# A two-block transformer on one core: the forget gates' columns go beside the rotated key's, and products of two heads alternate between array halves

## What is computed

```python
def _token_mixer(x, ...):
    z = x @ w_in                     # [256, 1024] @ [1024, N_IN]
    c_q, c_kv, k_rope, sb_qkv, conv_in, fox_qkv, fox_f, gate_logits = _split_cols(z)
    y_a = _mla(c_q, c_kv, k_rope, ...)                  # 4 heads, 96-wide queries and keys
    y_b = _stick_breaking(*_split_heads(sb_qkv))        # 4 heads of 64
    y_c = _conformer_conv(conv_in, ...)                 # 31 taps, a layer norm
    y_d = _forgetting_attention(*_split_heads(fox_qkv), fox_f, b_forget)
    gates = sigmoid(gate_logits + b_gate)
    merged = sum over branches of (y @ w_branch) * gates
    return merged @ w_o

def _forgetting_attention(q, k, v, forget_logit, b_forget):
    log_f = log_sigmoid(forget_logit + b_forget)        # 256 tokens, 4 heads
    c = cumsum(log_f)
    logits = q @ k * scale + c[query] - c[key]          # then causal softmax, then @ v
```

## Time and profile before

| | |
|---|---|
| median of 3 runs | 2617.33 us (2615.58 to 2617.4) |
| profiled execution | 2615.79 us, span of its instructions 2614.0 us |
| PE busy | 2441.6 us, 93% of the span |
| DVE, ACT busy | 676.6 us, 450.1 us |
| share of the chain that ended last | PE 71%, DMA 23%, DVE 3%, ACT 2% |
| third mixer, fourth mixer | about 1455 to 1700 us and 2033 to 2270 us of the span |

### The profile page before, as it was taken

The page is one execution under the profiler, slowest core; times in us unless marked ns, Lnnn a source line. Parts: engine busy times, 40 slices in busy tenths (PEclk is TensorE's granted clock), DMA queues, the critical chain, the costliest instruction groups (busy, mean ns, idle before and its releaser), DMA issues.

```text
span 2614.0 us, 28378 instructions
## 1 busy us (share of the span) xinstructions
PE 2441.6 (93%) x11488; PEld 1398.9 (54%) x11488; DVE 676.6 (26%) x1400; ACT 450.1 (17%) x814; POOL 0.2 (0%) x4
## 2 busy tenths in 40 slices
PE   7999999888889999988888999999999999999998
PEld 5775743333336673333333777774444777874443
DVE  3653321111003232101001533134112533042113
ACT  3141110000002121000000133102111242112111
POOL 0000000000000000000000000000000000000000
PEclk9999999999999999999999899999999999999999
DMA  9348669999997138999999532246999232148994
GB/s 402 132 188 366 250 282 428 428 429 428 428 427 289 73 129 335 429 428 428 429 428 427 215 129 97 97 192 239 425 422 416 110 129 97 65 193 331 426 421 187
DMA packets 53941, 769.64 MB, mean 294 GB/s; under 512 B 5984, under 2 KB 6496, under 8 KB 7008
## 3 DMA queue, kind: packets, MB, share of 16 engines
q1 hardware_dynamic: 53568, 768.17, 71.2%
q10 hardware_dynamic: 288, 0.26, 0.1%
HBM read 767.36 MB, written 1.05 MB: 294 GB/s over the span
## 4 chain that ended last, share of the span: by engine, by line
PE 71%; DMA 23%; DVE 3%; ACT 2%; issue 1%; SPq 0%; ACTq 0%; DVEq 0%
DMA slab<-in_experts 22%; PE psum L400 14%; PE psum L432 13%; PE psum L1930 8%; PE psum L1920 8%; PE psum L1967 7%; PE psum L1902 6%; PE psum L696 4%; PE psum L503 1%; DMA slab<-in_dense 1%; PE psum L1240 1%; PE psum L1953 1%; PE psum L626 0%; PE psum L1944 0%; PE psum L746 0%
## 5 line engine op out<-in xcount | busy, mean ns | idle before, releaser
L1920 PE MATMUL psum<-slab 128*64 128x512 f32 x2048 | 461.1, 597 | 77.6 <-DMA slab<-in_experts 73.8
L400 PE MATMUL psum<-slab 128*128 128x256 f32 (+6 forms) x1560 | 389.1, 406 | 12.2 <-ACT slab L2480 7.0
L1967 PE MATMUL psum<-slab 128*64 128x512 f32 x1536 | 359.5, 603 | 2.6 <-ACT slab L1998 2.6
L432 PE MATMUL psum<-slab 128*128 128x256 f32 x1504 | 345.4, 391 | 11.8 <-DVE slab L2770 6.6
L1920 PEld LDWEIGHTS psum<-slab 128*64 128x64 f32 x2048 | 142.1, 137 | 390.3 <-issue 274.7
L400 PEld LDWEIGHTS psum<-slab 128*128 128x128 f32 (+2 forms) x1560 | 272.9, 188 | 121.6 <-issue 70.6
L432 PEld LDWEIGHTS psum<-slab 128*128 128x128 f32 x1504 | 294.1, 196 | 60.9 <-issue 8.8
L1902 PE MATMUL psum<-slab 128*128 128x256 f32 x1024 | 249.3, 385 | 1.2 <-DVE slab L2020 1.2
L1930 PE MATMUL psum<-slab 128*64 128x512 f32 x1024 | 225.3, 592 | 0.0
L1902 PEld LDWEIGHTS psum<-slab 128*128 128x128 f32 x1024 | 183.2, 189 | 72.7 <-issue 50.3
L2010 DVE TENSOR_TENSOR slab<-psum,slab 128x512 f32<-128x512 f32 (+1 forms) x64 | 35.7, 558 | 691.6 <-PE psum L1920 502.3
(11 more groups left out here) (429 smaller groups left out, 1565.0 us busy)
## 6 DMA issues: line engine op xcount, KB each, us to landing
slab<-in_experts SPq DMA_DIRECT2D x288, 2048.0 KB, 20.2
slab<-in_dense SPq DMA_DIRECT2D x73, 2048.0 KB, 9.2
slab<-in_dense SPq DMA_DIRECT2D x2, 1680.0 KB, 16.8
slab<-in_vec SPq DMA_DIRECT2D x1, 2571.5 KB, 33.0
slab<-in_dense SPq DMA_DIRECT2D x1, 1328.0 KB, 27.6
slab<-in_dense SPq DMA_DIRECT2D x2, 640.0 KB, 13.9
slab<-in_xT SPq DMA_DIRECT2D x1, 1024.0 KB, 8.4
out<-slab SPq DMA_DIRECT2D x2, 512.0 KB, 2.6
```

The source lines that it names most:

```text
L400: ins = mm(out_ap, lhs, rhs, start=(n == 0), stop=(n == len(pairs) - 1), skip_group_check=True)
L432: ins = mm(psum[:, b, S * j:S * j + S], narrow(s, width)[:, k, c0 + P * j:c0 + P * j + P], src[:, k, :], start=(k == 0), stop=(k == KD - 1 ...
L1920: ins = mm(psum[CAP * e:CAP * e + CAP, n, :], xg[:, k, CAP * e:CAP * e + CAP], sl(w, KD)[:, e * (KD // 2) + i, :], start=(k == 0), stop=(k ...
L1967: ins = mm(psum[CAP * e:CAP * e + CAP, 2 + half, :], hidT[:, f, CAP * e:CAP * e + CAP], w, start=(f == 0), stop=(f == fc - 1), skip_group_ ...
```

## The change

1. Forget gates. They are computed with their four weight columns as the stationary side, into PSUM rows 0 to 3 of bank 3, and their eight products alternate with the eight of the rotated key. ACT copies the result, four rows of 256, to `lfr`. After the units of stick-breaking queries and keys two PE transposes turn it to tokens on partitions, as unit 7, and ACT copies it to `lf` as before. The list `MIX2_FREE` is unchanged.
2. Values of `mla` and `fox`: for each pair of heads (0 and 1, 2 and 3) both first products, then both second ones.
3. Logits of `mla` and `fox`: order of places 0, 2, 1, 3, which for `fox` is heads 0, 1, 2, 3.
4. Stick breaking: its logits' and values' products by pairs of heads in the same manner.

```diff
     def pe_logits(self, q, qk):
         for t in range(NT):
-            for j in range(H):
+            for j in (0, 2, 1, 3) if self.beside == 2 else range(H):
...
     def pe_values(self, q, v_of, out_of):
         q.e.wait_ge(sems["turned_read"], q.due("turned_read"))
-        for j in range(H):
-            h = self.order[j]
-            o = out_of(h)
-            mm(o, v_of(h, 0), self.pT[:, j, 0:2, :]...)
-            ins = mm(o[:, P:S], v_of(h, 1), self.pT[:, j, 2, :], ...)
+        for first in range(0, H, self.beside):
+            own = [list(self.order).index(h) for h in range(first, first + self.beside)]
+            for j in own:
+                h = self.order[j]
+                mm(out_of(h), v_of(h, 0), self.pT[:, j, 0:2, :]...)
+            for j in own:
+                h = self.order[j]
+                ins = mm(out_of(h)[:, P:S], v_of(h, 1), self.pT[:, j, 2, :], ...)
...
+lfr = view(MA0 + 3 * S, S)
...
 pe_mix2_in:
-    accumulate(psum[CH:96, b, S:2 * S], [(narrow(s, 420)[:, k, 384:416], xT[:, k, :]) for k in range(KD)])\
-        .then_inc(sems["unit_done"], 1)
-    b = u.bank()
-    for t in range(NT):
-        ins = accumulate(psum[:, b, H * t:H * t + H],
-                         [(xT[:, k, P * t:P * t + P], narrow(s, 420)[:, k, 416:420]) for k in range(KD)])
+    for k in range(KD):
+        for rows_, c0, n in ((slice(CH, 96), 384, 32), (slice(0, H), 416, H)):
+            ins = mm(psum[rows_, b, S:2 * S], narrow(s, 420)[:, k, c0:c0 + n], xT[:, k, :], start=(k == 0), stop=(k == KD - 1), ...)
     ins.then_inc(sems["unit_done"], 1)
     s = slot(q)
     for n in range(2):
         pe_features(u, s, xT, 2 * P * n)
+    b = u.bank()
+    u.need(4)
+    for t in range(NT):
+        ins = nc.tensor.transpose(psum[:, b, H * t:H * t + H], lfr[0:H, P * t:P * t + P], ident[0:H, 0:H])
+    ins.then_inc(sems["unit_done"], 1)
...
 act_mix2_in:
     A.activation(ckv, psum[:, 3, 0:S], ACT.Copy)
+    A.activation(lfr[0:H, :], psum[0:H, 3, S:2 * S], ACT.Copy)
...
-    act_unit(q, 4, lf, n=NT * H, shape=NT)
-    act_unit(q, 5, sbq, shape=2)
-    act_unit(q, 6, sbk, shape=2)
+    act_unit(q, 4, sbq, shape=2)
+    act_unit(q, 5, sbk, shape=2)
+    act_unit(q, 6, lf, n=NT * H, shape=NT)
...
 pe_sb:
-    for h in range(H):
-        half = slice(CH * (h % 2), CH * (h % 2) + CH)
-        mm(psum[:, h, 0:S], sbk[half, h // 2, 0:P], sbq[half, h // 2, :], start=True, stop=True)
-        ins = mm(psum[:, h, S:3 * P], sbk[half, h // 2, P:S], sbq[half, h // 2, P:S], start=True, stop=True)
+    for first in (0, 2):
+        for part in range(2):
+            for h in (first, first + 1):
+                half = slice(CH * (h % 2), CH * (h % 2) + CH)
+                ins = mm(psum[:, h, S * part:S + P * part], sbk[half, ...], sbq[half, ...], start=True, stop=True)
...
 dve_forget:
-    q.e.wait_ge(sems["lin_read"], q.due("lin_read", 3))
+    q.e.wait_ge(sems["lin_read"], q.due("lin_read", 5))
```

More of the change, by code:

```diff
@@ L732, in build, with __init__ @@
         class Attention:
-            def __init__(self, at, order, scale, turn=4, first=0):
+            def __init__(self, at, order, scale, turn=4, first=0, beside=1):
                 self.lg = view(at, NT, H, S)
@@ L738, in __init__ @@
                 self.nmax, self.sums = view(at + 3584, NT, H), view(at + 3592, NT, H)
-                self.order, self.scale, self.turn, self.first = order, scale, turn, first
+                self.order, self.scale, self.turn, self.first, self.beside = order, scale, turn, first, beside
             def pe_logits(self, q, qk):
                 for t in range(NT):
-                    for j in range(H):
+                    for j in (0, 2, 1, 3) if self.beside == 2 else range(H):
                         lhs, rhs = qk(j, t)
@@ L786, in pe_values @@
                 q.e.wait_ge(sems["turned_read"], q.due("turned_read"))
-                for j in range(H):
-                    h = self.order[j]
-                    o = out_of(h)
-                    mm(o, v_of(h, 0), self.pT[:, j, 0:2, :].rearrange("p a b -> p (a b)"), start=True, stop=False,
-                       skip_group_check=True)
-                    ins = mm(o[:, P:S], v_of(h, 1), self.pT[:, j, 2, :], start=False, stop=True, skip_group_check=True)
+                for first in range(0, H, self.beside):
+                    own = [list(self.order).index(h) for h in range(first, first + self.beside)]
+                    for j in own:
+                        h = self.order[j]
+                        mm(out_of(h), v_of(h, 0), self.pT[:, j, 0:2, :].rearrange("p a b -> p (a b)"), start=True, stop=False,
+                           skip_group_check=True)
+                    for j in own:
+                        h = self.order[j]
+                        ins = mm(out_of(h)[:, P:S], v_of(h, 1), self.pT[:, j, 2, :], start=False, stop=True, skip_group_check=True)
                 ins.then_inc(sems["attn_ready"], 1)
@@ L2354, in build @@
         MA0 = A0 + 8544
-        mla = Attention(MA0, range(H), 96.0 ** -0.5)
-        fox = Attention(MA0, (0, 2, 1, 3), CH ** -0.5)
+        mla = Attention(MA0, range(H), 96.0 ** -0.5, beside=2)
+        fox = Attention(MA0, (0, 2, 1, 3), CH ** -0.5, beside=2)
         sz, sl_, sn = (view(MA0 + 1536 * j, H, 3 * P) for j in range(3))
         mla_sq = view(MA0, 3, S)
+        lfr = view(MA0 + 3 * S, S)
         mt = view(MA0, 2, H, S)
@@ L2377, in pe_mix2_in @@
             accumulate(psum[:, b, 0:S], [(narrow(s, 420)[:, k, 256:384], xT[:, k, :]) for k in range(KD)])
-            accumulate(psum[CH:96, b, S:2 * S], [(narrow(s, 420)[:, k, 384:416], xT[:, k, :]) for k in range(KD)])\
-                .then_inc(sems["unit_done"], 1)
-            b = u.bank()
-            for t in range(NT):
-                ins = accumulate(psum[:, b, H * t:H * t + H],
-                                 [(xT[:, k, P * t:P * t + P], narrow(s, 420)[:, k, 416:420]) for k in range(KD)])
+            for k in range(KD):
+                for rows_, c0, n in ((slice(CH, 96), 384, 32), (slice(0, H), 416, H)):
+                    ins = mm(psum[rows_, b, S:2 * S], narrow(s, 420)[:, k, c0:c0 + n], xT[:, k, :], start=(k == 0), stop=(k == KD - 1),
+                             skip_group_check=True)
             ins.then_inc(sems["unit_done"], 1)
@@ L2606, in pe_sb @@
             q.e.wait_ge(sems["attn_read"], q.due("attn_read"))
-            for h in range(H):
-                half = slice(CH * (h % 2), CH * (h % 2) + CH)
-                mm(psum[:, h, 0:S], sbk[half, h // 2, 0:P], sbq[half, h // 2, :], start=True, stop=True)
-                ins = mm(psum[:, h, S:3 * P], sbk[half, h // 2, P:S], sbq[half, h // 2, P:S], start=True, stop=True)
+            for first in (0, 2):
+                for part in range(2):
+                    for h in (first, first + 1):
+                        half = slice(CH * (h % 2), CH * (h % 2) + CH)
+                        ins = mm(psum[:, h, S * part:S + P * part], sbk[half, h // 2, P * part:P * part + P], sbq[half, h // 2, P * part:],
+                                 start=True, stop=True)
             ins.then_inc(sems["sb_pre"], 1)
@@ L2622, in pe_sb @@
             q.e.wait_ge(sems["sb_prob"], q.due("sb_prob"))
[L2623 to L2627, removed]
+            for first in (0, 2):
+                for t in range(NT):
+                    for h in (first, first + 1):
+                        o = branch_out(h)
+                        ins = mm(o[:, P * t:], vsf[:, t, CH * h:CH * h + CH], sz[:, h, S * t:S + P * t], start=(t == 0), stop=(t == 1),
+                                 skip_group_check=True)
             ins.then_inc(sems["attn_ready"], 1)
@@ L2757, in dve_merge @@
         def dve_merge(q, l):
-            q.skip("lin_read", 11)
+            q.skip("lin_read", 9)
             q.skip("unit_done", 16)
```

## The result

| | before | changed kernel |
|---|---|---|
| median, same chip, 7 runs each | 2615.58 us | 2604.15 us (2596.92 to 2607.76) |
| ratio | | 0.9948 (95%: 0.9933 to 0.9963) |
| profiled execution | 2615.79 us | 2599.33 us |
| mean granted clock over its span | 0.985 | 0.989 |

The change saves 13.6 us by the ratio (9.7 to 17.5), where 11.4 was forecast. The time forecast, 2605.9 us, lies 1.8 us above the median of the seven runs. So there is something to explain on both counts: what the sum got right, and why single executions of one program lie 10.8 us apart.

A forecast was written before the change was run, and what follows sets the result against it. PE was taken as the bound, by the chain in order of time. In-projection 9.6, values 1.3 and 0.2, logits 0.3 sum to 11.4 us: 2615.79 to 2604.4, plus 1.5 for the median, 2605.9 us; range 2602.5 to 2611.

The forecast's parts named there:

- the low end: Whole kernel: 2602.5 us, from 1.6 us more by values, logits and transposes and 1.7 us more by the clock.
- a fall of the clock avoided once more, at half of the 3.4 us: In-projection clock: 1.7 us beyond the sum, half of the 3.4 us (1.2 + 2.2) that one fall cost.
- In-projection, 9.6 us: Third and fourth mixers: moved forget gates save 6.5 us and 3.1 us, of which 2.2 us is clock in the third.
- The gates are free beside the key: In-projection: sixteen gate rows run at once with the rotated key's sixteen, stretch stays 3.7 us; bound 3.5 us each mixer.
- second rival: In-projection: gates' products don't run beside the key's, 3.5 us come back twice, gain 4.4 us, 2612.9 us; chance 0.07.
- Program order: Values and stick-breaking logits: if matmuls run strictly in turn, 5.2 us gained instead of 1.8, 2602.5 us; not adopted.
- Transposes: In-projection: two PE transposes of the gates cost 0.6 us together (bounds 0.3 and 1.0), their wait nothing.
- fourth rival: Slower: PE waits at the transposes or `mla_norm` for ACT and DVE, 8.3 us in each mixer, 2622.5 us; chance 0.03.
- `fox` values: Attention: the new head order brings them from 2.17 to 1.51 us, 0.66 us in each mixer, 1.3 us.
- `fox` logits: Attention: drop from 2.11 to about 1.8 us but give nothing; PE's idle time before L778 grows.
- third rival: Experts: the gain is lost where transfers run at a share of 0.98, time near 2617 us; chance 0.05.
- First rival: In-projection: the clock gives nothing back, 1.2 + 2.2 us are lost, gain 8.0 us, 2609.3 us; chance 0.24.

The follow-up runs named there:

- run of the pairs alone: The kernel before with only the new order of heads in values and logits, forget gates unchanged; 2612.8 us, ratio 0.9989.
- runs in blocks: Changed kernel, key and gate products alternating in blocks: eight products 2608.28 us, two 2603.27 us, four 2602.7 us.
- run in blocks: Changed kernel with the eight products of the rotated key first, then the eight of the gates; 2608.28 us, ratio 0.9974.
- on one tile: Changed kernel with the gates' products on the rotated key's array columns, result in another PSUM bank; 2609.5 us, ratio 0.9976.

## Why the sum came out, and why the low end did not hold

The mechanism was right, and the sum of the work holds. What failed is the low end, 2602.5 us, and in it one step: "a fall of the clock avoided once more, at half of the 3.4 us", 1.7 us, as all that the clock could give beyond the sum. The profiled execution, which is also the median of the first three, lies 3.2 us below it. Its span is 16.3 us shorter than that of before: 9.6 + 1.4 + 0.4 = 11.4 of the terms that I had, 3.2 by falls that are missing at the two `fox` waits, 2.5 by a clock that comes back sooner in the 96 rows ahead of the latent key, less 0.9 in the rest. The step allowed 1.7 us for what was 5.7 in this execution. Of that, much is luck: over seven executions the median is 2604.15 us, inside the range.

- **In-projection, 9.6 us: right.** It is 6.48 + 3.16 = 9.6 in the profiled pair. Elsewhere it is split otherwise: the run of the pairs alone takes 1504.40 - 1476.72 = 27.68 us where the changed kernel takes 22.84, 4.8 in each mixer, 9.7 in both. I had read one mixer with a fall of 3.4 us and one with none; two other profiles have some 1.7 in each. The sum is the same by chance of the one profile I had.
- **The gates are free beside the key: right**, 3.59 us for both, 7.04 on one tile. The Trainium skill says in "TensorE: Matmul & The Clock Gate", Part 3, that a weight load overlaps a running matmul only where the row groups differ. Both tiles here have the same 128 rows and overlap almost wholly; the measurement decides against this sentence of the Trainium skill, and with it falls my second rival.
- **Program order.** The same Part of the Trainium skill has matmuls start strictly in turn. The runs in blocks show rows starting ahead of up to three others of another tile. That fits `mla`'s values, whose second head stands four rows behind the first: head by head they took 1.51 us before and had next to nothing to gain, 1.45 after. The time that this rule gave, 2602.5 us, is within the scatter of the runs; its pieces are not, since the six values' products and the stick-breaking logits gained 1.4 + 0.4 us in all and not 5.2. (The expectation of the run in blocks read a reach of eight rows from `mla`; four is enough for what it shows.)
- **Transposes**: 0.41 us in each mixer (0.6 forecast), and no wait ahead of them. DVE waited 3.35 us for ACT before the norm in the fourth mixer, against the 3.7 of slack that I worked out from the earlier trace rows. The fourth rival had no ground.
- **`fox` values** 1.4 us (1.3), **`fox` logits** nothing: PE's idle time before L778 went from 1.00 to 1.11 us in the timeline, fourth mixer.
- **Experts**: from the start of the third mixer's merge to the fourth mixer it is 379.4 us after and 380.0 before. The merge's 256 rows take 57.4 and 58.7 of it, so the experts are 0.7 us longer, 322.0 against 321.3. That is all that was lost there, and the third rival fell.
- **First rival** (the clock gives nothing back): fell. Without the four-column products, no dense stretch of the in-projection is slow in 20 mixers.
- **What was off: the clock's term and the low end.** The step "a fall of the clock avoided once more, at half of the 3.4 us" counted falls in the in-projection only, from one profile. There are more places, and they vary, as the 96 rows do, which the sum leaves out. The fall at the `fox` wait stood in my own chain of before and I did not price it. It costs 1.5 to 1.7 us, came in every mixer with four-column products and in half of those without: 2 x 1/2 x 1.6 = 1.6 us on the average. The work terms and the in-projection's clock as measured are 9.7 + 1.4 + 0.4 = 11.5; with 1.6 they are 13.1, beside 13.6 measured (9.7 to 17.5). The low end should have reached some 5 us further down, since executions of the changed kernel differ by 10.8 us: their mean clock goes from 0.985 to 0.989, and 0.004 x 2600 = 10.4, an estimate that takes the whole span as PE's.

What stays open: why the falls at the `fox` wait are rarer once the gates' products have changed, some 120 us ahead of it. The counts show it (8 of 8 against 9 of 18), no run was made that tells a cause from a run of luck. In all 17 the clock fell close to PE's return, from 0.4 us ahead of the start of L778 to 0.9 us behind it. Open too is why the clock comes back sooner or later in the 96 rows ahead of the latent key, which take between 22.4 and 24.1 us in these profiles.

## What to carry to other kernels

Products that fill few array columns should go to column tiles of their own and stand within four rows of another tile's: then they cost nothing here, in any order within that reach, and there is little left to gain by alternating what already is that close. A run of products that stream only a few columns (16 of them here) mostly costs more than its own time, since the rows behind it run at half clock for a while (7 of 8 mixers); turned round, with the few columns as the stationary side, this went away. Before pricing the clock from one profile, look for all pieces of equal rows with unequal times, in several executions: each is a term, with a frequency.

## What the runs showed of the chip

- The clock can fall from 2.4 to 1.2 GHz with PE busy at 1.00 throughout: dense rows took 15.45 to 16.14 us for 14.07 behind 16 or 32 four-column products in 7 of 8 mixers, and in none of 20 without them.
- A row on another column tile starts beside the row that stands four places before it, ahead of the three between, and no earlier: the stretch takes 3.59 us in blocks of four rows, 4.50 in blocks of eight, 6.20 in blocks of sixteen, 7.04 on one tile.
- The scatter of the changed kernel's executions, 10.8 us of 2604, goes with that of its mean granted clock, 0.985 to 0.989.
